# Two-part rotary queries stacked in one operand: latent attention of a two-layer block on one Trainium2 core

## The reference

```python
def mla_layer(x, pos, norm_g, w_in, q_norm_g, w_q_up, kv_norm_g, w_kv_up, q_gain, k_gain, w_out):
    z = rms_norm(x, norm_g) @ w_in
    cq, ckv, k_pe, gate = jnp.split(z, [512, 1024, 1088], axis=-1)
    q = (rms_norm(cq, q_norm_g) @ w_q_up).reshape(b, s, 16, 192)
    kv = (rms_norm(ckv, kv_norm_g) @ w_kv_up).reshape(b, s, 16, 128 + 128)
    k_nope, v = kv[..., :128], kv[..., 128:]
    k = jnp.concatenate([k_nope, broadcast(k_pe, 16 heads)], axis=-1)   # 128 + 64
    q, k = rms_norm(q, q_gain), rms_norm(k, k_gain)
    q, k = (concatenate([t[..., :128], rope(t[..., 128:], pos)]) for t in (q, k))
    o = mla_attend(q, k, v, pos)     # softmax(q k^T / sqrt(192), chunk mask) v
    return x + (o * silu(gate)) @ w_out
```

## Time and profile before

| | |
|---|---|
| median of 3 runs | 3488.89 us (3486.98 to 3489.59) |
| the profiled execution | 3493.14 us, of which the span is 3491.3 us |
| PE busy | 3354.6 us, 96% of the span |
| DVE, ACT, POOL busy | 44%, 20%, 60% |
| mean granted clock of TensorE | 0.977 of full speed |

### The profile page before, as it was taken

The page is one execution under the profiler, slowest core; times in us unless marked ns, Lnnn a source line. Parts: engine busy times, 40 slices in busy tenths (PEclk is TensorE's granted clock), DMA queues, the critical chain, the costliest instruction groups (busy, mean ns, idle before and its releaser), DMA issues.

```text
span 3491.3 us, 63813 instructions
## 1 busy us (share of the span) xinstructions
PE 3354.6 (96%) x21506; PEld 2669.3 (76%) x21506; DVE 1536.4 (44%) x3118; ACT 695.4 (20%) x1260; POOL 2095.6 (60%) x3492
## 2 busy tenths in 40 slices
PE   8999999998999989899989998999999999999899
PEld 6777777777888867678867776787888888788687
DVE  3444444435666663651156666214332343323410
ACT  2111111102323220220023333102111121111200
POOL 6444444445767658688743433687676666666566
PEclk9999999999999989899999999999999999999999
DMA  4111111112222213233311111232222222222232
GB/s 149 50 50 50 50 48 45 50 50 67 72 72 72 72 49 90 69 85 96 88 49 36 39 36 36 70 93 84 77 78 78 72 72 78 78 72 75 63 103 78
DMA packets 459580, 239.43 MB, mean 69 GB/s; under 512 B 27902, under 2 KB 456121, under 8 KB 458937
## 3 DMA queue, kind: packets, MB, share of 16 engines
q1 hardware_dynamic: 455656, 232.19, 22.9%
q10 hardware_dynamic: 3792, 5.28, 0.4%
HBM read 233.22 MB, written 4.19 MB: 68 GB/s over the span
## 4 chain that ended last, share of the span: by engine, by line
PE 87%; DVE 5%; issue 3%; POOL 2%; ACT 2%; SPq 1%; DMA 0%; DVEq 0%; ACTq 0%; POOLq 0%; PEldq 0%
PE proj L321 23%; PE proj L322 21%; PE proj L323 21%; POOL w_lo L311 2%; PE work L2278 2%; PE work L1924 2%; PE work L321 1%; PE work L1114 1%; PE work L323 1%; PE work L322 1%; PE work L656 1%; PE work L670 1%; PE work L664 1%; PE work L1917 1%; PE work L630 1%
## 5 line engine op out<-in xcount | busy, mean ns | idle before, releaser
L307 POOL TENSOR_SCALAR w_hi<-raw_weights 128x256 fp32r<-128x256 f32 x1744 | 746.3, 455 | 1379.9 <-PE proj L323 1364.3
L311 POOL TENSOR_TENSOR w_lo<-raw_weights,w_hi 128x256 fp32r<-128x256 f32 x1744 | 1365.4, 814 | 0.0
L321 PE MATMUL proj<-x_hi,w_hi 128*128 128x512 f32 x2976 | 1236.5, 415 | 37.8 <-POOL w_lo L311 11.0
L322 PE MATMUL proj<-x_lo,w_hi 128*128 128x512 f32 x2976 | 1185.4, 398 | 0.0
L323 PE MATMUL proj<-x_hi,w_lo 128*128 128x512 f32 x2976 | 1184.3, 398 | 0.0
L321 PEld LDWEIGHTS proj<-x_hi,w_hi 128*128 128x128 f32 x2976 | 564.6, 190 | 203.8 <-issue 47.3
L323 PEld LDWEIGHTS proj<-x_hi,w_lo 128*128 128x128 f32 x2976 | 564.4, 190 | 138.6
L322 PEld LDWEIGHTS proj<-x_lo,w_hi 128*128 128x128 f32 x2976 | 566.3, 190 | 117.0 <-issue 2.2
L321 PE MATMUL proj<-o_hi,w_hi 128*128 128x512 f32 x256 | 103.6, 405 | 7.2 <-POOL w_lo L311 3.6
L321 PE MATMUL proj<-lat_hi,w_hi 128*128 128x512 f32 x224 | 99.5, 444 | 7.6 <-DVE lat_lo L1733 4.0
L322 PE MATMUL proj<-o_lo,w_hi 128*128 128x512 f32 x256 | 101.8, 398 | 0.0
(11 more groups left out here) (462 smaller groups left out, 4296.0 us busy)
## 6 DMA issues: line engine op xcount, KB each, us to landing
raw_weights<-w_in SPq DMA_DIRECT2D x260, 256.0 KB, 3.2
raw_weights<-b_w_in SPq DMA_DIRECT2D x256, 256.0 KB, 3.1
raw_weights<-a_w_in SPq DMA_DIRECT2D x100, 256.0 KB, 3.2
raw_weights<-w_out SPq DMA_DIRECT2D x64, 256.0 KB, 3.0
raw_weights<-a_w_out SPq DMA_DIRECT2D x64, 256.0 KB, 3.0
raw_weights<-b_w_out SPq DMA_DIRECT2D x64, 256.0 KB, 3.0
raw_weights<-a_w_kv_up SPq DMA_DIRECT2D x32, 256.0 KB, 2.8
mix<-x SPq DMA_DIRECT2D x4, 1024.0 KB, 8.0
```

What stands on the lines that cost most here:

```text
L307: pool.tensor_scalar(part(hi_v, s % 2, q), part(raw_v, s, q), 1.0, 1.0, ALU.mult, ALU.mult).then_inc(hi_done, 1)
L311: pool.tensor_tensor(part(lo_v, s % 2, q), part(raw_v, s, q), part(hi_v, s % 2, q).bitcast(F32), ALU.subtract).then_inc(w_split, 1)
L321: pe.matmul(out, w_h, a_h, start=start, stop=False)
L322: pe.matmul(out, w_h, a_l, start=False, stop=False)
```

## The change

A rotary tile has 64 rows for each head and its product used all 128 rows, half of them zero on the key's side, three times a block. Now the query's high part stands in the rows of its own head and its low part in the rows of the other one (`q_rope[h]`), and the key's high part stands in both halves. One matmul then gives high times high and low times high, and a second one high times low: two instead of three. Score blocks take five matmuls instead of six.

Beside it the order is changed. Of the 28 parts 20 stand among the heads and 8 behind. Six stand ahead of S0 instead of four, and two instead of one in steps 1 and 2. `rot` stands right behind the last V and writes to `work1` instead of `work3`. The value tiles are copied from PSUM by ACT instead of DVE. Of DVE's low parts only three stand ahead of the first scores (`lq0`, `lqr0`, then `lk0` and `lkr0` as before), and `lq1`, `lk1`, `lqr1`, `lkr1` follow in steps 0, 1, 2 and 3. DVE copies tile 0 of the next pair in step 7, tile 1 in step 8, and tiles 2 and 3 in step 9. Indentation is cut in the diff.

```diff
...
 MA_PE = steps("mla_pe", "rot rows sums vt0 inv0 inv1 vt1 " + piped("S{0}", "T{0}", "V{0}"))
-MA_ACT = steps("mla_act", "sq2 sq0 sq1 sq3 sq4 rows hq0 hq1 hqr vt0 vt1 hk0 hkr0 hk1 hkr1 " + piped("e{0}", "pT{0}", ""))
-MA_DVE = steps("mla_dve", "qc qs qrr ms msk " + RSQRT + " lq0 lq1 lqr k0 kr0 lk0 lkr0 k1 kr1 " +
+MA_ACT = steps("mla_act", "sq2 sq0 sq1 sq3 sq4 rows hq0 hqr0 hqr1 hq1 vt0 vt1 hk0 hkr0 hk1 hkr1 " + piped("e{0}", "pT{0}", ""))
+MA_DVE = steps("mla_dve", "qc qs qrr ms msk " + RSQRT + " lq0 k0 kr0 lqr0 lk0 lkr0 k1 kr1 " +
                piped("sc{0} nb{0}", "rec{0} p{0}", "g{0}", (1, 0, 2))
-               .replace("nb1", "nb1 lk1").replace("nb2", "nb2 lkr1"))
+               .replace("nb0", "nb0 lq1").replace("nb1", "nb1 lk1").replace("nb2", "nb2 lqr1").replace("nb3", "nb3 lkr1"))
...
 m_sq, sq_parts = zip(*(take_m(f"sq{n}") for n in range(5)))
-q_hi, qr_hi, k_hi = sq_parts[0:2], sq_parts[2], sq_parts[3:5]
+q_hi, k_hi = sq_parts[0:2], sq_parts[3:5]
 m_qg = a8.take("mla_q_rope_gained", SEQ)
-m_qr, qr_lo = take_m("q_rope")
+m_qr = a8.take("mla_q_rope", SEQ)
 m_kr = a8.take("mla_k_rope", SEQ)
-m_tmp = a8.take("mla_tmp", SEQ)
+m_tmp, tmp_part = take_m("tmp")
+q_rope = (sq_parts[2], tmp_part)
...
+MLA_AHEAD = 20
...
     pe.wait_ge(LN2_DVE.sem, LN2_DVE.done(f"lo{2 * LB - 1}"))
-    run(part, 4)
+    run(part, 8)
     mla_scale_pe(pe, 0, part)
-    pe.wait_ge(kr_zeroed, 4)
+    pe.wait_ge(kr_zeroed, 2)
...
             used += parts
-        run(part, 16 - used)
+        run(part, MLA_AHEAD - used)
...
     need = lambda steps, name: pe.wait_ge(steps.sem, steps.done(name, p))
-    run(part, 4)
+    run(part, 20 - MLA_AHEAD)
+    pe.wait_ge(tile_free, T_MLA + 7 * p + 3)
+    pe.matmul(work[1][:, :], common[:, C_ROT:C_ROT + P], m_qg[:, :], start=True, stop=True)\
+      .then_inc(MA_PE.mark("rot"), 1)
+    run(part, 3)
     pe.wait_ge(MA_DVE.sem, MA_DVE.after(p))
-    pe.wait_ge(tile_free, T_MLA + 7 * p + 3)
-    pe.matmul(work[3][:, :], common[:, C_ROT:C_ROT + P], m_qg[:, :], start=True, stop=True)\
-      .then_inc(MA_PE.mark("rot"), 1)
-    run(part, 2)
-    run(part, 1)
...
     need = lambda steps, name: pe.wait_ge(steps.sem, steps.done(name, p))
-    yield 4
+    yield 6
...
             multiply(pe, work[k % 2][:, :], q_hi[h][:, qs], q_lo[h][:, qs], k_hi[h], k_lo[h], True, False)
-            multiply(pe, work[k % 2][:, :], qr_hi[:, qs], qr_lo[:, qs], kr_hi[h], kr_lo[h], False, True)\
-                .then_inc(MA_PE.mark(f"S{k}"), 1)
-            yield 1
+            pe.matmul(work[k % 2][:, :], q_rope[h][:, qs], kr_hi[h], start=False, stop=False)
+            pe.matmul(work[k % 2][:, :], q_rope[h][:, qs], kr_lo[h], start=False, stop=True)\
+              .then_inc(MA_PE.mark(f"S{k}"), 1)
+            yield 2 if k in (1, 2) else 1
...
     act.activation(m_e[0][:, :], work[2][:, :], ACT.Copy).then_inc(MA_ACT.mark("rows"), 1)
+    def take_values(h):
+        act.wait_ge(tile_free, T_MLA + 7 * p + 5 + h)
+        tile_done(act, U_MLA + 4 * p + UNIT_OF[5 + h])
+        act.activation(m_vr[h][:, :], proj[(5 + h) % 4][:, :], ACT.Copy).then_inc(tile_free, 1)
+    take_values(0)
     high = lambda out, x, name: act.activation(out, x, ACT.Copy).then_inc(MA_ACT.mark(name), 1)
-    need(MA_PE, "sums")
+    high(q_hi[0], m_q[0][:, :], "hq0")
+    need(MA_DVE, "qrr")
     for h in range(2):
-        high(q_hi[h], m_q[h][:, :], f"hq{h}")
-    need(MA_DVE, "qrr")
-    high(qr_hi, m_qr[:, :], "hqr")
+        high(q_rope[h][HEADS[h], :], m_qr[HEADS[h], :], f"hqr{h}")
+    high(q_hi[1], m_q[1][:, :], "hq1")
...
         act.activation(m_vt[h][:, :], work[h][:, :], ACT.Copy).then_inc(MA_ACT.mark(f"vt{h}"), 1)
+        if h == 0:
+            take_values(1)
     for h in range(2):
-        hs = HEADS[h]
...
         need(MA_DVE, f"kr{h}")
-        high(kr_hi[h][hs, :], m_kr[hs, :], f"hkr{h}")
+        high(kr_hi[h], m_kr[:, :], f"hkr{h}")
...
 def mla_dve(dve):
-    take_q_and_k(dve, 0)
+    take_q_and_k(dve, 0, range(4))
     for h in range(2):
-        for part in (kr_hi[h], kr_lo[h]):
-            dve.memset(part[HEADS[1 - h], :].bitcast(F32), 0.0).then_inc(kr_zeroed, 1)
+        dve.memset(kr_lo[h][HEADS[1 - h], :].bitcast(F32), 0.0).then_inc(kr_zeroed, 1)
     with dve.Fori(0, A_HEADS // 2 - 1) as p:
-        mla_heads_dve(dve, p, lambda: take_q_and_k(dve, p + 1))
-    mla_heads_dve(dve, A_HEADS // 2 - 1, lambda: None)
+        mla_heads_dve(dve, p, lambda tiles: take_q_and_k(dve, p + 1, tiles))
+    mla_heads_dve(dve, A_HEADS // 2 - 1, lambda tiles: None)
...
 def take_tile(dve, p, j):
+    if j == 0:
+        dve.wait_ge(tile_free, T_MLA + 7 * p)
...
         tile_done(dve, U_MLA + 4 * p + UNIT_OF[j])
-    dst = (m_q[0], m_q[1], m_qg, m_k[0], m_k[1], m_vr[0], m_vr[1])[j][:, :]
+    dst = (m_q[0], m_q[1], m_qg, m_k[0], m_k[1])[j][:, :]
...
-def take_q_and_k(dve, p):
-    for j in range(4):
+def take_q_and_k(dve, p, tiles):
+    for j in tiles:
...
     need(MA_PE, "rot")
-    done(dve.tensor_tensor(m_tmp[:, :], work[3][:, :], sin[:, :], ALU.mult), "qs")
+    done(dve.tensor_tensor(m_tmp[:, :], work[1][:, :], sin[:, :], ALU.mult), "qs")
...
     done(dve.tensor_tensor(m_qr[:, :], m_qr[:, :], m_tmp[:, :], ALU.add), "qrr")
-    take_tile(dve, p, 5)
...
     rsqrt(dve, MA_DVE, p, work[3][:, 0:32], m_small[:, 16:32], m_small[:, 32:48], rs)
-    take_tile(dve, p, 6)
...
                                 f"kr{h}")
+    low_q = lambda h: low(q_lo[h], m_q[h][:, :], q_hi[h], f"q{h}")
+    low_q_rope = lambda h: low(q_rope[h][HEADS[1 - h], :], m_qr[HEADS[h], :], q_rope[h][HEADS[h], :], f"qr{h}")
+    low_q(0)
     for h in range(2):
-        low(q_lo[h], m_q[h][:, :], q_hi[h], f"q{h}")
-    low(qr_lo, m_qr[:, :], qr_hi, "qr")
-    for h in range(2):
-        hs = HEADS[h]
...
                                       ALU.mult, ALU.mult), f"k{h}")
-        done(dve.tensor_tensor(m_kr[hs, :], k_rope[hs, :], work[2 + h][hs, :], ALU.mult), f"kr{h}")
+        if h:
+            dve.wait_ge(MA_DVE.sem, MA_DVE.done("lkr0", p))
+        done(dve.tensor_tensor(m_kr[:, :], k_rope[:, :], work[2 + h][:, :], ALU.mult), f"kr{h}")
         if h == 0:
+            low_q_rope(0)
...
                                           rs[:, k:k + 1], ALU.mult, ALU.mult), f"nb{k}")
+        if k == 0:
+            low_q(1)
...
         if k == 2:
+            low_q_rope(1)
+        if k == 3:
             low_k_rope(1)
-        if k == HB + 1:
+        if k >= HB - 1:
             chain()
-            take_next()
+            take_next((0,) if k == HB - 1 else (1,) if k == HB else (2, 3))
```

## The result

The changed kernel takes 3447.47 us (median of 4 runs, 3445.53 to 3448.51), the kernel before 3487.93 us in the same set: ratio 0.9884, 95% interval 0.9867 to 0.9901. That is 40.5 us faster, where 43.9 were forecast, and 2.5 us above the forecast time. The profiled execution took 3445.53 us with a span of 3443.7 us.

What follows compares the result with a forecast made beforehand. PE, busy 96% of the span, was taken as the bound. Gains of 6.05 us in each of pairs 0 to 5, 4.75 in pair 6 and 2.9 in the last make 43.9 us: 3445.0 us, range 3438 to 3461.

Steps and rivals of the forecast that it cites:

- The matmuls: Score blocks: eight rotary matmuls less per pair, each 0.233 us on PE's path, gain 1.87 us a pair.
- The gap at S0: PE's wait for `lkr0` in the loop closes with 0.22 us to spare, gaining 2.55 us a pair.
- the first rival: S0's gap stays in part, `lkr0` 1 us late and low clock behind it: 28.8 us gained, 3460 us; chance 12%.
- The low clock: Behind S0 in the loop it goes with the gap: 1.64 us in pairs 0 to 5, 0.34 us in pair 6.
- From S0 to T1: Start of each loop pair: T0 about 4.4 us after S0 without wait, T1 reached 7.4 us after S0.
- Waits in steps 0 to 3: Low parts slowed beside POOL cost PE 0.3 us a pair, within bounds of 0 and 2.0 us.
- The second rival: Saved time returns as waits in steps 0 to 3, 2.0 us a loop pair: 32.0 us gained, 3457 us; chance 11%.
- Step 8: T7 no longer starts late, tile 0's copy fits in step 7: gain 0.29 us a pair, bounds 0 and 0.3.
- `rot` behind V7: End of a loop pair: `rot`, without four parts ahead, is still covered with 0.9 us while tile 2 gets ready.
- the slower case: Rival: PE stops at `rot` for 2.4 us with low clock behind, S0's stop stays: 10.3 us lost, 3499 us; chance 2%.
- The last pair: Pair without parts as cover: earlier `lkr0`, one matmul less in S0 and shorter steps, together 2.9 us gained.
- The score steps of 2.73 us: Last pair: steps fall from 2.88 us to the DVE and ACT loop's 2.73 us, gaining 1.1 us.

Runs made afterwards that it cites:

- e_stack: Against the changed kernel: order of work and 16 parts as before, only the stacked queries (two rotary matmuls) kept, `lqr1` in step 3; 3472.18 us, ratio 0.9958 to the kernel before.
- e_parts16: Changed kernel with 16 parts among the heads as before: four ahead of S0, one in each step; 3459.64 us, ratio 0.9934 to the kernel before.
- e_both: Changed kernel with `lq1` ahead of the first scores, the other three low parts one step earlier, and tile 0 copied in step 5; 3437.45 us.
- e_lkr1: Changed kernel with only the low parts moved one step earlier, tile 0's copy left in step 7; one execution, 3439.61 us.
- second profile: The changed kernel unchanged, timed once more in more rounds and profiled again; 3445.59 us against 3485.52 us for the kernel before.

## Why the prediction was right, and where it was off

**The matmuls.** Right: lines 1907 and 1908 start 0.23 us apart, 64 instructions fewer. Alone they gave 0.9 to 1.3 us a pair at like clocks (`e_stack`) of the 1.87 counted, since T0, T1 and S4 then waited.

**The gap at S0.** Right in kind. `lkr0` was to come 1.37 us earlier. From the last instruction of the inverse roots (1836.77) to its end (1841.91) it took 5.14 us; before, it was 1855.12 - 1848.18 = 6.94 us, so 1.80 us. The rest is `lk0`, which started at 1839.98, 0.2 us ahead of POOL's second half, and took 0.78 us instead of 1.22. That is luck: nothing in the prediction counts on it. So the margin was larger than the 0.22 us counted: S0 started at 1842.74, 0.83 us behind the end of `lkr0`, and the first rival (3460 us) had no ground. (The rival's sum also has 1 us of gap left, where its own late `lkr0` of 1 us less the margin of 0.22 leaves 0.78.) `e_parts16` shows that without the two parts S0 waits.

**The low clock.** Right: 1.00 in the loop.

**From S0 to T1.** Right: 4.38 us to T0, no wait at T1, though `lqr1` took 1.19 us beside POOL. `lk1` in step 1 took 0.93 us (0.69 in `e_both`), and T1 was still on time.

The prediction read the 1.20 us of a subtraction beside POOL, against 0.69 alone, as a partial block. The rows show a full one. First `lqr1` of the changed kernel with the POOL piece beside it, then `lk0` and `lkr0` of the kernel before with theirs:

```profile
1850.97 0.72 POOL L311 TENSOR_TENSOR w_lo<-raw_weights,w_hi 128x256 fp32r<-128x256 f32 x1
1851.05 1.19 DVE L2038 TENSOR_TENSOR mla_tmp_part<-mla_q_rope,mla_tmp_part 64x512 fp32r<-64x512 f32 x1
...
1852.73 0.72 POOL L311 TENSOR_TENSOR w_lo<-raw_weights,w_hi 128x256 fp32r<-128x256 f32 x1
1852.78 1.22 DVE L2029 TENSOR_TENSOR mla_k_part<-mla_k,mla_sq_part 128x512 fp32r<-128x512 f32 x1
1853.41 1.17 POOL L311 TENSOR_TENSOR w_lo<-raw_weights,w_hi 128x256 fp32r<-128x256 f32 x1
1853.92 1.20 DVE L2029 TENSOR_TENSOR mla_k_rope_lo<-mla_k_rope,mla_k_rope_hi 64x512 fp32r<-64x512 f32 x1
```

Each subtraction ends 0.54 to 0.55 us behind the end of the POOL piece that was running when it started (1852.24 behind 1851.69, 1854.00 behind 1853.45, 1855.12 behind 1854.58), with 64 rows as with 128. The POOL piece that started at 1853.41, beside `lk0`, is stretched in its turn: 1.17 us instead of 0.72, ending 0.58 us behind `lk0`. So the later one waits for the rest of the earlier one. A subtraction takes 0.69 us alone and at most 1.23 us in the loops of the two kernels. The rule of the Trainium skill (SBUF — State Buffer, section "Who interferes with whom"), that the instruction that comes second is blocked until the first is through, is what these rows show. What the prediction worked out from it, a wait for a whole piece and 0.5 us a pair, was too much per instruction: `lqr1` waited for the rest of a piece of 0.72 us and was 0.50 us longer for it. How 0.5 us a pair follows from two such waits the prediction doesn't work out.

**Waits in steps 0 to 3: mis-sized.** The prediction took 0.3 us a pair, a value chosen between its bounds of 0 and 2.0 us, and argued that from step 2 on PE's block (3.2 us) is longer than DVE's step (2.73 us). S4 was late by 0.79 us. What failed is the sentence that the four low parts stand where DVE otherwise waits: `lkr1` in step 3 stands behind the scores of block 3, which stand behind the division, and it is needed by the very next S. The kernel before had it one step earlier, which the prediction doesn't mention. It had no place to be late in, and it had a late start (`lqr1` of 1.19 us, and 0.38 us instead of 0.16 for the small instruction ahead). The second rival was the right one in its mechanism, at 0.5 us a pair over the forecast rather than 1.7. The prediction's own sign of being wrong, an idle stretch ahead of S4, is there.

**Step 8: the wrong consumer.** I counted 0.29 us of gain, since T7 would no longer wait, and put tile 0's copy beside the scores at no cost. T7 indeed doesn't wait (T7 follows the parts at 1870.04). But tile 4 goes into tile 0's bank, and its first part waits for that copy: 0.36 us. I checked the copy against DVE's next work and not against who waits for the bank. `e_lkr1` against `e_both` shows 0.4 us for it (45.37 and 44.96 us a pair).

The two together: 0.79 + 0.36 = 1.15 us a pair where 0.3 stood, 0.85 us more. 6.05 - 0.85 = 5.20 us; pairs 1 to 5 show 51.4 - 46.2 = 5.2 us. Over the seven pairs that is 35 us instead of 41.1.

**`rot` behind V7.** Right: no wait ahead of it in any pair, so the slower case had nothing in it. **The last pair** was to gain 2.9 us. It took 44.3 us in the first profile and 42.6 us in the second, against 45.4 us before (all up to the next stage's first copy), so it gained 1.1 and 2.8 us. Of the 1.7 us between the two profiles 0.6 us is S0, which started 14.58 us behind `rot` in the first and 13.98 us in the second, since DVE's subtractions fell otherwise against POOL's pieces (`lkr0` took 1.21 and 0.87 us). The other 1.1 us is behind S0, where the granted clock differs:

```profile
2118.80:2129.00 10.20, 8.99 (x26) 6.89 (x27) 6.70 (x18) 3.53 (x7) 2.34 (x3) 0.50 0.17 52
```

```profile
2121.10:2124.50 3.40, 3.29 (x8) 2.61 (x9) 1.99 (x5) 1.23 (x2) 2.63 (x4) 0.55 0.05 15
2124.50:2134.70 10.20, 7.88 (x45) 5.95 (x44) 8.30 (x24) 5.08 (x11) 0.00 (x0) 0.98 0.18 52
```

The first is the first profile, where the clock is the low one for 10.2 us, from 0.5 us ahead of S0 on; the other two lines are the second profile, where it is the low one for some 3 us. Nothing in the program differs between them.

The score steps of 2.73 us, a sign of being right, did not come. DVE's scores of blocks 0 and 7, first profile and second:

```profile
2122.01 0.69 DVE L2070 CUSTOM_DVE_ANT_0 mla_scores<-work,masks 128x512 f32<-128x512 f32 x1 [1.58 <-PE work L1908]
...
2142.97 0.69 DVE L2070 CUSTOM_DVE_ANT_0 mla_scores<-work,masks 128x512 f32<-128x512 f32 x1 [0.18 <-DVE mla_probs L2065]
...
2123.70 0.69 DVE L2070 CUSTOM_DVE_ANT_0 mla_scores<-work,masks 128x512 f32<-128x512 f32 x1 [1.38 <-PE work L1908]
...
2143.76 0.69 DVE L2070 CUSTOM_DVE_ANT_0 mla_scores<-work,masks 128x512 f32<-128x512 f32 x1 [0.18 <-DVE mla_probs L2065]
```

A step is 20.96 / 7 = 2.99 us in the first and 20.06 / 7 = 2.87 us in the second, against 2.88 before: the 1.1 us counted for PE's shorter block is not there. That the second profile nearly has the 2.9 us forecast is luck: S0 came 2.4 us earlier than before instead of 1.37.

**The sum.** 37 us in the stage against 43.9, the 6 us of the two waits being most of the difference. The measured 40.5 us is nearer to the forecast than the stage is, by 3 us that I can't place and that the interval allows. So it is luck in part that the time came within 2.5 us of the forecast; the loop's gain was 6 us too high.

## What to carry to other kernels

When work is moved into idle time of an engine, ask for each moved instruction which instruction waits for it next, and how far away that is; a slot that is idle on average is no slot if its result is due at once. Count the buffers too: when a projection is moved ahead, the copy that frees its PSUM bank is on the path, and the one that waits for it is the matmul that reuses the bank, not a reader of the copy. And when a matmul is taken out of a loop that stops elsewhere, the order that closes the stop can be worth more than the matmul: here 27 against 13 us.

## What was not expected of the hardware

The same stop of PE, 2.4 us ahead of S0, was followed by the low clock in some pairs and not in others of one execution: pairs of 50.0 and of 49.3 us in the kernel with only the stacked queries. Stops of 0.2 to 0.6 us were not followed by it in the loops of three kernels (the changed one, and those with the third matmul and with 16 parts), where the granted clock is 1.00 over all seven pairs. A stop of 3.0 to 3.6 us ahead of the last pair's S0 was followed by it at S0 for 10.2 us in one profile of the changed kernel and for some 3 us in the other, and in `e_lkr1` not at S0 at all, but 5 us later.

DVE's subtractions and POOL's pieces of the low weights (line 311) exclude each other for whole instructions: in the loops of both kernels a subtraction that starts beside such a piece ends 0.54 to 0.55 us behind the piece's end, wherever in the piece it started.
